# A sparse-attention stage between two projections: new order, masks by TensorE, and two of four products on GpSimd

## What is computed

```
p = rms_norm(h) @ w_in                    # q, kc, vc, ks, vs, kw, vw, gates, bg, cg, hd
o_c = masked softmax(q . compressed k) . compressed v   # 15 windows of 32 tokens, two-layer MLP with gelu
o_s, o_w = causal softmax(rope(q) . rope(ks or kw)) . (vs or vw)   # 8 heads each
yc = g0 * o_c + g1 * o_s + g2 * o_w       # sigmoid gates
yd = bg * causal_conv3(cg * hd)
h = h + concat(yc, yd) @ w_out
```

## Time and profile before

| | us |
|---|---|
| median of 3 runs | 2113.72 |
| the runs | 2109.43, 2114.61, 2113.72 |
| the profiled execution's own time | 2109.94 |
| its span | 2107.9 |
| PE busy | 2016.6 (96%) |
| DVE busy | 1577.1 (75%) |
| ACT busy | 1150.0 (55%) |
| POOL busy | 394.0 (19%) |

### The profile page before, as it was taken

One profiled execution on the slowest core, in us unless ns is written; L12 is line 12 of the kernel. 1 busy time (PEld: TensorE's weight loads), 2 busy tenths in 40 slices (PEclk: granted clock), 3 DMA queues, 4 the chain that ended last, 5 costly groups with the idle time before them and its releaser, 6 DMA issues.

```text
span 2107.9 us, 31941 instructions
## 1 busy us (share of the span) xinstructions
PE 2016.6 (96%) x11820; PEld 1767.6 (84%) x11820; DVE 1577.1 (75%) x2176; ACT 1150.0 (55%) x1687; POOL 394.0 (19%) x192
## 2 busy tenths in 40 slices
PE   7999999999999999999999999999987999999997
PEld 6888987888888889888889998888975888888885
DVE  6777886677777769677778666777785588888887
ACT  5445543554454455554455535445445577777775
POOL 2222003232222310122322432223000300000000
PEclk9999999999999999999999999999998999999999
DMA  8555520455645554355544005555451588888895
GB/s 341 186 194 169 179 90 15 169 197 187 196 167 197 180 187 152 120 179 195 184 170 150 2 15 182 185 194 192 160 180 39 180 331 327 325 327 325 325 329 190
DMA packets 73395, 401.22 MB, mean 190 GB/s; under 512 B 8256, under 2 KB 8384, under 8 KB 41152
## 3 DMA queue, kind: packets, MB, share of 16 engines
q1 hardware_dynamic: 72848, 398.07, 54.1%
q10 hardware_dynamic: 432, 1.57, 0.2%
HBM read 398.57 MB, written 1.05 MB: 190 GB/s over the span
## 4 chain that ended last, share of the span: by engine, by line
PE 76%; DVE 13%; PEld 4%; ACT 3%; issue 2%; POOL 0%; DMA 0%; SPq 0%; ACTq 0%; PEldq 0%; DVEq 0%; POOLq 0%
PE psum L744 18%; PE psum L306 13%; PE psum L307 13%; PE psum L308 13%; PE psum L748 9%; DVE w_lo L290 4%; PE psum L969 2%; PE psum L957 2%; ACT w_hi L283 1%; PE psum L2803 1%; DVE w_lo L296 1%; PE psum L320 1%; PEld psum L306 1%; PEld psum L308 1%; PEld psum L307 1%
## 5 line engine op out<-in xcount | busy, mean ns | idle before, releaser
L290 DVE TENSOR_TENSOR w_lo<-ring,w_hi 128x1024 fp32r<-128x1024 f32 x498 | 742.7, 1521 | 179.4 <-ACT w_hi L283 178.0
L283 ACT ACTIVATE w_hi<-ring 128x1024 fp32r<-128x1024 f32 x744 | 739.9, 1051 | 234.2 <-PEq L500 129.1
L296 POOL TENSOR_TENSOR w_lo<-ring,w_hi 128x1024 fp32r<-128x1024 f32 x132 | 324.0, 2455 | 1079.7 <-ACT w_hi L283 1079.7
L744 PE MATMUL psum<-fT,w_hi 128*128 128x512 f32 x1760 | 422.4, 391 | 12.9 <-DVE w_lo L290 10.5
L744 PEld LDWEIGHTS psum<-fT,w_hi 128*128 128x128 f32 x1760 | 329.6, 188 | 84.3 <-issue 7.6
L306 PE MATMUL psum<-w_hi,hT_hi 128*128 128x384 f32 (+4 forms) x896 | 321.7, 359 | 12.4 <-POOL w_lo L296 4.0
L308 PE MATMUL psum<-w_hi,hT_lo 128*128 128x384 f32 (+4 forms) x896 | 310.7, 347 | 0.0
L307 PE MATMUL psum<-w_lo,hT_hi 128*128 128x384 f32 (+4 forms) x896 | 310.3, 346 | 0.0
L306 PE MATMUL psum<-w_hi,act_hi 128*128 128x512 f32 x616 | 242.4, 394 | 5.5 <-DVE act_lo L842 4.6
L307 PE MATMUL psum<-w_lo,act_hi 128*128 128x512 f32 x616 | 241.2, 392 | 0.0
L308 PE MATMUL psum<-w_hi,act_lo 128*128 128x512 f32 x616 | 239.9, 390 | 0.0
(11 more groups left out here) (485 smaller groups left out, 2413.9 us busy)
## 6 DMA issues: line engine op xcount, KB each, us to landing
ring<-in_stream SPq DMA_DIRECT2D x249, 1024.0 KB, 5.4
ring<-in_stream SPq DMA_DIRECT2D x248, 512.0 KB, 4.3
tables<-in_tables SPq DMA_DIRECT2D x1, 2261.0 KB, 19.9
gain_row<-in_gains ACTq DMA_DIRECT2D x3, 512.0 KB, 3.7
rows<-in_rows SPq DMA_DIRECT2D x1, 1288.0 KB, 22.6
X<-in_x SPq DMA_DIRECT2D x1, 1024.0 KB, 5.0
result<-X SPq DMA_DIRECT2D x2, 512.0 KB, 3.3
columns<-in_columns SPq DMA_DIRECT2D x1, 993.0 KB, 15.0
```

Of the source, the lines that this page charges most:

```text
L283: act.activation(part(w_hi, g, i), ring[:, k, i * PART:(i + 1) * PART], ACT.Copy) \
L290: dve.tensor_tensor(part(w_lo, g, i), ring[:, k, i * PART:(i + 1) * PART], part(w_hi, g, i).bitcast(F32), ALU.subtract) \
L296: pool.tensor_tensor(part(w_lo, g, 2), ring[:, k, 2 * PART:STEP], part(w_hi, g, 2).bitcast(F32), ALU.subtract) \
L744: pe.matmul(psum[:, 4 + 2 * (s % 2) + o, :], w[0][:, o, k, :], fT[:, k, :, :].rearrange("p a c -> p (a c)"), start=k == 0, stop=False, ski ...
```

## The change

The sparse stage gets another order, another layout in memory and other helpers. `masked_max_vector` and `masked_exp_scalar` read the scores in PSUM; the mask is added by one bf16 product of PE per unit; scores of group 0 are made between steps 5 and 6, and the transposes of rotated q and k after step 4. cg is scaled by rstd squared and hd is multiplied by it as it leaves PSUM, so the weight columns of bg come last. n_S is two halves in the parity that the first output step does not use; group 0's exponentials lie in O. DVE makes all third pieces of w_lo up to the first output step's. POOL multiplies groups 2 and 3 by gate over sum. The three runs of `keep_warm` in the stage are gone. The convolution's half of the first output step is multiplied ahead of the rest (`conv_part`).

```diff
-                b = open_bank(pe, f"{name} {s} {j}")
+                b = bank(f"{name} {s} {j}") if (s, j) in begun else open_bank(pe, f"{name} {s} {j}")
...
-                for k in range(KT):
+                ks = range(tiles if (s, j) in begun else KT)
+                for k in ks:
...
-                                           [x[:, k, 0:c] for x in w], k == 0, k == KT - 1)
+                                           [x[:, k, 0:c] for x in w], k == 0 and (s, j) not in begun, k == ks[-1])
...
+                if (s, j) == (row_at, 0):
+                    row_vector(dve, at, bank(f"norm {at} row"))
+                    row_kept = True
...
-                scales = place(s, j, rstd_row) if kind != "k" else places_
+                if kind == "k":
+                    scales = places_
+                elif scale_of is not None:
+                    scales = scale_of(dve, s, j)
+                else:
+                    scales = place(s, j, rstd_row)
...
+        def masked_max_vector(dve, stage, name, units, scale, small):
+            for i, u in enumerate(units):
+                dve.wait_ge(*after(f"{u}"))
+                dve.tensor_reduce(small[:, i, :], bank(u)[:, 0:UNIT].rearrange("p (b c) -> p b c", c=P), AX.X, ALU.max).then_inc(*stage.vector())
+            dve.wait_ge(*stage.vector.so_far())
+            dve.tensor_tensor(small[:, :, 1], small[:, :, 1], small[:, :, 2], ALU.max).then_inc(*stage.vector())
+            dve.wait_ge(*stage.vector.so_far())
+            dve.tensor_scalar(small[:, :, 0:2], small[:, :, 0:2], -scale, None, ALU.mult).then_inc(*stage.vector(f"{name} max"))
...
+        def masked_exp_scalar(act, stage, name, units, S, scale, less, sums):
+            act.wait_ge(*after(f"{name} max"))
+            for i, u in enumerate(units):
+                for t, cols in enumerate((slice(0, P), slice(P, UNIT))):
+                    act.activation(S[:, i, cols], bank(u)[:, cols], ACT.Exp, scale=scale, bias=less[:, i, t:t + 1], accum_out=sums[:, i, t:t + 1]) \
+                       .then_inc(*stage.scalar(f"{name} exp"))
+                marks[f"used {u}"] = marks[f"{name} exp"]
...
-        def scores_tensor(pe, stage, label, q, k):
+        def scores_tensor(pe, stage, label, q, k, masked=False):
...
-            pe.matmul(b[:, 0:P], q[:, 0:P], k[:, 0:P], start=True, stop=True)
-            pe.matmul(b[:, P:UNIT], q[:, P:SEQ], k, start=True, stop=True).then_inc(*stage.tensor(label))
+            pe.matmul(b[:, 0:P], q[:, 0:P], k[:, 0:P], start=True, stop=not masked, skip_group_check=masked)
+            ins = pe.matmul(b[:, P:UNIT], q[:, P:SEQ], k, start=not masked, stop=not masked, skip_group_check=masked)
+            if masked:
+                ins = pe.matmul(b[:, 0:UNIT].rearrange("p (b c) -> p b c", c=P)[:, 0::2, :], ident_bf16, bias_bf16[:, 0::2, :],
+                                start=False, stop=True, skip_group_check=True)
+            ins.then_inc(*stage.tensor(label))
...
-            n_S = take("n_S", [P, 16, UNIT])
...
+            out_parity = (first_step[[n for n, (kind, _) in enumerate(NETWORK) if kind == "sparse"][0]] + SPARSE_K + SPARSE_T + SPARSE_C) % 2
+            n_half = []
+            for n in range(2):
+                for parity in range(2):
+                    if parity != out_parity:
+                        n_half.append(take(f"n_S{n}", [P, 8, UNIT]))
+                    else:
+                        take(f"n_unused{n}", [P, STEP])
...
+        n_S0 = O_flat[:, 0:4 * UNIT].rearrange("p (u c) -> p u c", u=4)
...
-            return [((n_bg, n_cg, n_hd)[c // 4 - 1][:, c % 4, :], b[:, 0:SEQ])]
+            if 8 <= c < 12:
+                return [(n_pad[:, c % 4, 2:2 + SEQ], b[:, 0:SEQ])]
+            return [((n_cg, None, n_bg)[c // 4 - 1][:, c % 4, :], b[:, 0:SEQ])]
...
+        def n_scale(eng, s, j):
+            c = 3 * (s - SPARSE_K) + j
+            if 4 <= c < 8:
+                return [(None, n_row2)]
+            if 8 <= c < 12:
+                eng.wait_ge(*after(n_tile(c - 4)))
+                return [(None, n_cg[:, c % 4, :])]
+            return n_place(s, j, rstd_row)
...
-            proj_tensor(pe, "sparse", g0, N_KINDS, at, between={2: turn_plain})
+            def turn_rotated():
+                for t in range(TT):
+                    pe.wait_ge(*after(f"sparse rope {t}"))
+                    b = open_bank(pe, f"sparse qr {t}")
...
+            def scores(i):
+                pe.wait_ge(*after("used sparse kt 1"))
+                for u in range(4 * i, 4 * i + 4):
+                    s = u % SLOTS8
+                    scores_tensor(pe, sparse, f"sparse s {u}", n_qr[slot_rows(s), s // 2, :], n_kt[slot_rows(s), u // SLOTS8, :], masked=True)
...
+            def turn_units(i):
+                for u in range(4 * i, 4 * i + 4):
+                    turn_unit_tensor(pe, sparse, f"sparse pt {u}", n_exps(i)[:, u % 4, :], f"sparse p {i}")
+            def products(i, ts=range(TT)):
+                for u in range(4 * i, 4 * i + 4):
+                    pe.wait_ge(*after(f"used sparse pt {u}"))
+                    br, s = divmod(u, SLOTS8)
+                    for t in ts:
+                        for j, pt in enumerate(unit_blocks(n_unit(u), t)):
+                            v = (VS, VW)[br] + 64 * (s % 2)
+                            pe.matmul(bank(f"sparse o {t}")[:, 64 * s:64 * s + 64], pt, n_tok[:, j, v:v + 64], start=u == 0 and j == 0, stop=False,
+                                      skip_group_check=True)
+            def finish(t):
+                pe.wait_ge(*after("used sparse vcmp"))
+                pe.wait_ge(*after(f"used sparse pct {t}"))
+                pe.matmul(bank(f"sparse o {t}"), n_pct[:, t, :], n_vcmp.rearrange("p s d -> p (s d)"), start=False, stop=True,
+                          skip_group_check=True).then_inc(*sparse.tensor(f"sparse o {t}"))
+            proj_tensor(pe, "sparse", g0, N_KINDS, at, between={2: turn_plain, 4: turn_rotated, 5: lambda: scores(0)})
...
-                        keep_warm(pe, b, 0 if which else 11)
...
-            for t in range(TT):
-                pe.wait_ge(*after(f"sparse rope {t}"))
...
+            scores(1)
...
-            scores(range(0, 4))
+            turn_units(0)
...
-            scores(range(4, 8))
+            scores(2)
...
-            scores(range(8, 16))
...
-            for i in range(4):
-                turn_units(i)
-            pe.wait_ge(*after("sparse pc"))
+            turn_units(1)
+            scores(3)
+            turn_units(2)
             for t in range(TT):
                 b = open_bank(pe, f"sparse pct {t}")
+                pe.wait_ge(*after("sparse pc"))
...
-                b = open_bank(pe, f"sparse o {t}")
...
-            out_tensor(pe, "sparse", at, 4, warm=16)
+                open_bank(pe, f"sparse o {t}")
+            for i in range(3):
+                products(i)
+            turn_units(3)
+            products(3, (0,))
+            finish(0)
+            products(3, (1,))
+            finish(1)
+            g = g0 + len(N_KINDS) + SPARSE_C
+            w = [x[:, g % 2, :].rearrange("p (k c) -> p k c", k=KT) for x in (w_hi, w_lo)]
+            def conv_part(t):
+                b = open_bank(pe, f"sparse out 0 {t}")
+                wait_split(pe, g)
+                pe.wait_ge(*after("sparse conv"))
+                for k in range(4, KT):
+                    three_passes(pe, b[:, 0:COLS], [x[:, k, t * P:(t + 1) * P] for x in (hT_hi, hT_lo)], [x[:, k, 0:COLS] for x in w], k == 4, False)
+            conv_part(0)
+            turn_tensor(pe, "sparse", sparse, 4, [f"used sparse o {t}" for t in range(TT)], ts=(0,))
+            conv_part(1)
+            turn_tensor(pe, "sparse", sparse, 4, [f"used sparse o {t}" for t in range(TT)], ts=(1,))
+            out_tensor(pe, "sparse", at, 4, begun=((0, 0), (0, 1)))
...
-            proj_copies_scalar(act, "sparse", at, N_KINDS, n_place, {2: plain}, ahead=True)
+            def gate():
+                wait_proj(act, "sparse", N_KINDS, range(SPARSE_K))
+                does("sparse gate", n_gate.rearrange("p t b s -> p t (b s)"), n_tok[:, :, GL:GL + 24], ACT.Sigmoid)
+                act.activation(warm[:, :], eps, ACT.Exp)
...
+            def rotated():
+                for t in range(TT):
+                    act.wait_ge(*after(f"sparse qr {t}"))
...
+            def exps(i):
+                if i == 1:
+                    act.wait_ge(*after("sparse hid 1"))
+                mine = slice(4 * i, 4 * i + 4)
+                masked_exp_scalar(act, sparse, f"sparse {i}", N_GROUPS[i], n_exps(i), 64 ** -0.5, n_max[:, mine, :], n_sum[:, mine, :])
...
+            def turned_units(i):
+                for u in range(4 * i, 4 * i + 4):
+                    act.wait_ge(*after(f"sparse pt {u}"))
+                    does(f"used sparse pt {u}", n_unit(u), bank(f"sparse pt {u}")[:, 0:UNIT], ACT.Copy)
...
+            proj_copies_scalar(act, "sparse", at, N_KINDS, n_place, {2: plain}, ahead=True,
```

(82 more changed lines are left out.)

140 lines of the change are left out of this document (52 added, 88 removed).

## The result

The change made the kernel slower by a quarter of a per cent, where a gain of 14 us, 0.7%, was forecast.

A forecast was written before the change was run, and what follows sets the result against it. The sparse stage was taken as bound by the order of its work. Savings of 0.2 by the compression's start, 0.6 within it, 12.5 to F and 0.6 in the tail gave 14.0: 2109.9 to 2095.9 us (2097.9 from the mean), range 2090 to 2107.

The forecast's parts named there:

- Projection and compression: Start of the sparse stage: -0.2 us at the compression's start and -0.6 within it.
- The rstd row: Projection: the row is copied at step 1, so PE's wait for it goes, -2.9 us.
- The stall for the tile (7, 1): Projection step 7: the tile waits for unit 0's bank, freed by ACT's first exponentials behind a split, +2.0 us.
- The third step of the compression: Compression: its split by DVE ends at 1564.7, its products at 1567.5, against 1568.3.
- The price of a score unit: Scores: four units take 1.78 us without a mask, a bf16 mask product about 0.12 each, a group 2.2.
- The clock in the middle: PE's products up to F: one more us because the clock is low after the wait for group 2.
- the rival in which it isn't given back: Clock stays at half until F: products cost 13 us more, gain 1, 2111, no change; chance 0.06.
- F: End of the products with v, forecast at 1609.8 against 1623.15 before.
- "Largest": Groups 1 to 3: four reductions from PSUM at 0.47 us, with two small ones 2.4 against 4.1; bounds 2.2 and 3.0.
- POOL's product: Groups 2 and 3, gate over sum on POOL: 3.8 us for 1536 elements, upper bound 7.6; DVE takes 1.76.
- The wait forecast for largest 3 behind POOL's lock: Group 3: largest's two small steps blocked while POOL works, ready at 1590.7 and not 1588.8, 1.9 us lost.
- The tail: F to output step 1: 12.8 us, a new PE stall of 3.4, 2.1 lost at half clock; 14.9 against 15.5.

The follow-up runs named there:

- the kernel before without its 12: The kernel before without the 12 unread 512-column products ahead of the last eight units' transposes; 2110.43 us, ratio 0.9991.
- last + split + 8 + 12: Kernel after with masks behind each group's four units, output step 1's split earlier, 8 and 12 unread products ahead of groups 0 and 2's transposes; 2092.01 us, 0.9913.
- last + split + 8: Kernel after with masks behind each group's four units, output step 1's split earlier, 8 unread products ahead of group 0's transposes; 2100.34 us, ratio 0.9934.

## Why the prediction was wrong, point by point

**Projection and compression: right, but for one term.** The rstd row is not waited for. The stall for the tile (7, 1) came as said, 1.77 for 2.0. The third step of the compression began at 1566.47 and not at 1564.7. The difference, 1.8, is about that of the four score units, 4.3 with their masks for the 2.2 in the sum.

**The price of a score unit: the first step that failed.** The sum took the row of four units without a mask (1.78) and added the masks as four bf16 products of 0.12. Both rows were right; adding them was wrong, because the 1.78 was the time of pairs that overlap, and the mask between them takes the overlap away. 1.06 instead of the 0.55 of the sum for each of 16 units; shown by the kernels with the masks last (2.15 for four).

**The clock in the middle: the step that decided.** The prediction gave the middle one us for the clock, and a chance of 0.06 to the rival in which it isn't given back, because "twice it returned under steady work, and the products are steady". The two returns were at 1588.9, where unmasked scores ended and transposes began, and at 1606.0, under products of `keep_warm`. (The first came 5.8 us after PE's work began, not 6.4: 0.60 over 7.2 us is 5.8 us at half.) From that the prediction made a rule for steady work of any kind. In the kernel after PE worked from 1578.88 to 1606.5 without a stop, and the clock came back only at 1606.3, in the transposes of group 2; then it was lost 1.3 us into the 72 products, also without a stop, and returned at 1626.8. The arithmetic against the forecast F of 1609.8: products began at 1608.4 and not at 1594.3 (+14.1, of which 1.8 came with the compression's start and 2.0 are group 1's scores; the 10.3 left over is put to the stretch at half clock with eight score units in it); the 72 products took 14.4 and not 9.2 (+5.2); the transposes of group 3 took 2.8 and not 1.4 (+1.4). Together +20.7, and F was 1630.5. In that stretch the clock is the larger part. Its eight units took 15.1; at full clock, an estimate from the rows above, they would take 8.5 with the masks between them and 4.3 with them last. With the masks last and the clock at half for only 6.8 us (1583.3 to 1590.1) F came at 1610.9, with 4.65 us of unread products in it. That is near the forecast 1609.8; the unread products and the 6.8 us weren't in the sum, so its other terms were, if anything, on the long side.

**"Largest", exponentials, POOL.** The reductions took 0.56 for 0.47 assumed. POOL's product took 2.75 and 3.60 for 3.8, inside the bounds of 1.76 and 7.6. The wait forecast for largest 3 behind POOL's lock did not come: its reductions ended at 1604.5, PE being late, when POOL had been done for 3 us. What did show is the other side of the lock. Beside DVE's "sparse conv" (1609.05, 1.22 long, two SBUF inputs) POOL's product, begun at 1609.27, took 0.85 longer than the one that ran alone. The Trainium skill ("SBUF — State Buffer", "SBUF: two separate sides") has the pair locked for the whole instruction; 0.85 of the 1.0 left of DVE's agrees about. In all fourteen kernels with POOL's products it is the same: 2.75 or 2.76 for the one, 3.60 for the one that begins 0.22 behind that instruction of DVE.

**The tail: right in length, short in what follows.** F + 12.9 for F + 12.8, the stall 3.68 for 3.4, the clock fell behind it and cost 1.7 for 2.1 assumed. Not in the sum was that the clock falls again at the entrance of the experts, where 14 unread products took 6.04 us instead of 3.18; with the rows around them 3.0 more. So 4.7 at the start of output step 1 (1643.4 for 1638.7), 1.7 and 3.0 are 9.4, the 9.5 by which the profiled executions differ.

**Which rival it was.** The rival of the clock in the middle named the mechanism. Its price (13 more, no change) was put on the products and transposes behind the wait, which lost 6.6 against the sum, and nothing on the scores and compressed scores ahead of it, where most was lost. The prediction had read the level of 0.60 and 0.54 in bursts as a matter of idle times alone, and took "no idle time" for "full clock".

**What stays open.** Why the clock stays at half through some unbroken work and comes back under other is not settled. It came back under unread bf16 products, under transposes (24 of them, 1609.1 in the kernel before without its 12) and also under 64-row scores (1590.1 in "last + split + 8 + 12"), so the shape alone doesn't tell, and no run varied it alone. Nor does any run separate what the idle times ahead of the 72 products do from the state that they meet. The spread of 16 us of "last + split + 8" does go with the clock: over its ten runs the mean granted clock falls from 0.993 (2088.3) to 0.983 (2104.6), nearly in step with the time. What sends one run one way and the next another is open.

## What to carry to other kernels

Before an instruction is added between others, ask whether the duration in the trace is of one alone or of several that overlap; on TensorE keep products over 64 rows next to each other and put those over 128 rows behind them. A removed filler or a filled wait changes what the clock does to everything behind it, so price the following stretch at both levels, and don't take unbroken work for full clock. Look at the level directly ahead of a long run of small products: here 8 unread products at that place gained 3.8 us. When weights' splits stand behind table loads and copies in a queue, moving one up can be worth more than the stall it shows (5.3 us of the tail for a stall of 3.7, since the clock fell behind the stall).
